# Opening stage of a two-block transformer kernel: modulation as columns on transposed tiles, unit weights by piece, masks by ScalarE and VectorE

## What is computed

```python
# block 1
mod = silu(c) @ w_mod + b_mod                     # 6 rows of 1024: sh1, sc1, gt1, sh2, sc2, gt2
h = layer_norm(x) * (1.0 + sc1) + sh1
proj = h @ w_in                                    # xbc, dt, q, k, v, f, z and two gates
xbc = silu(causal_depthwise_conv(xbc, conv_w, conv_b))
# block 2, used much later, depends on positions only
mod_2 = silu(c_2) @ w_ada + b_ada                  # 6 rows more
bias = bias_table[t5_bucket(pos_k - pos_q)]        # 32 buckets, 24 heads, 256 x 256 each
```

## Time and profile before

| | |
|---|---|
| median of 3 runs | 2214.21 us |
| the profiled execution's own time | 2215.75 us |
| its span, first to last instruction | 2213.9 us |
| mean granted TensorE clock | 0.873 |
| TensorE matmul busy | 1644.6 us (74%) |
| VectorE, ScalarE, GpSimd busy | 440.2, 287.3, 104.3 us |
| DMA | 670.55 MB, mean 303 GB/s |

### The profile page before, as it was taken

The page is one execution under the profiler, slowest core; times in us unless marked ns, Lnnn a source line. Parts: engine busy times, 40 slices in busy tenths (PEclk is TensorE's granted clock), DMA queues, the critical chain, the costliest instruction groups (busy, mean ns, idle before and its releaser), DMA issues.

```text
span 2213.9 us, 19952 instructions
## 1 busy us (share of the span) xinstructions
PE 1644.6 (74%) x8097; PEld 860.0 (39%) x8097; DVE 440.2 (20%) x890; ACT 287.3 (13%) x602; POOL 104.3 (5%) x99
## 2 busy tenths in 40 slices
PE   6899999979998699999998744655464544554444
PEld 2575654444443477687754411311121111211111
DVE  6430542342222322121325300000000000000001
ACT  6211222020000222121223100000000000000000
POOL 7000000000000100111111000000000000000000
PEclk9999999979999799999999777877778766877777
DMA  8899444729998342443452479999999999999995
GB/s 276 293 340 341 178 157 142 295 90 429 426 429 316 128 152 78 166 138 133 137 169 105 200 335 428 428 427 429 427 429 427 428 427 428 427 429 427 428 427 247
DMA packets 116171, 670.55 MB, mean 303 GB/s; under 512 B 8643, under 2 KB 11400, under 8 KB 85360
## 3 DMA queue, kind: packets, MB, share of 16 engines
q1 hardware_dynamic: 111568, 657.50, 73.3%
q0 software_dynamic: 3744, 11.11, 1.7%
q10 hardware_dynamic: 768, 0.64, 0.1%
HBM read 661.88 MB, written 7.34 MB: 302 GB/s over the span
## 4 chain that ended last, share of the span: by engine, by line
PE 61%; DMA 31%; DVE 3%; ACT 2%; issue 2%; SPq 1%; POOL 0%; DVEq 0%; ACTq 0%; POOLq 0%
PE psum L914 13%; PE psum L904 12%; DMA ring<-in_w_up 10%; DMA ring<-in_w_down 10%; PE psum L1403 10%; DMA ring<-in_w_gate 9%; PE psum L1217 5%; PE psum L1247 3%; PE psum L872 2%; PE psum L1187 2%; PE psum L1257 1%; PE psum L1143 1%; SPq L643 1%; PE psum L1340 1%; PE psum L1277 1%
## 5 line engine op out<-in xcount | busy, mean ns | idle before, releaser
L1403 PE MATMUL psum<-work,prob 128*32 128x512 f32 x1024 | 286.5, 724 | 159.0 <-DMA ring<-in_w_up 83.9
L1403 PE MATMUL psum<-ring,prob 128*32 128x512 f32 x1024 | 286.5, 724 | 151.1 <-DMA work<-in_w_up 86.2
L914 PE MATMUL psum<-ring,hT 128*128 128x512 f32 x672 | 303.8, 597 | 4.7 <-ACT hT L177 2.9
L904 PE MATMUL psum<-hT,ring 128*128 128x256 f32 x1152 | 277.2, 385 | 1.6 <-DVE hT L177 1.6
L904 PEld LDWEIGHTS psum<-hT,ring 128*128 128x128 f32 x1152 | 213.7, 193 | 36.3 <-issue 10.6
L1403 PE MATMUL psum<-work,hT 128*32 128x512 f32 x512 | 138.4, 703 | 88.8 <-DMA ring<-in_w_down 88.8
L1403 PE MATMUL psum<-ring,hT 128*32 128x512 f32 x512 | 138.4, 703 | 55.6 <-DMA work<-in_w_down 54.0
L914 PEld LDWEIGHTS psum<-ring,hT 128*128 128x128 f32 x672 | 123.9, 191 | 135.7 <-issue 129.1
L1403 PEld LDWEIGHTS psum<-work,prob 128*32 128x32 f32 x1024 | 70.7, 131 | 261.7 <-issue 261.7
L1403 PEld LDWEIGHTS psum<-ring,prob 128*32 128x32 f32 x1024 | 70.6, 131 | 253.1 <-issue 253.1
L177 ACT ACTIVATE work<-psum 128x512 f32<-128x512 f32 (+2 forms) x99 | 56.0, 566 | 608.3 <-PE psum L1389 236.5
(11 more groups left out here) (322 smaller groups left out, 1581.1 us busy)
## 6 DMA issues: line engine op xcount, KB each, us to landing
ring<-in_w_gate SPq DMA_DIRECT2D x40, 2048.0 KB, 19.2
work<-in_w_up SPq DMA_DIRECT2D x40, 2048.0 KB, 20.4
work<-in_w_gate SPq DMA_DIRECT2D x40, 2048.0 KB, 20.4
ring<-in_w_up SPq DMA_DIRECT2D x40, 2048.0 KB, 20.7
ring<-in_w_down SPq DMA_DIRECT2D x40, 2048.0 KB, 19.8
work<-in_w_down SPq DMA_DIRECT2D x40, 2048.0 KB, 20.0
ring<-in_w_in SPq DMA_DIRECT2D x72, 1024.0 KB, 7.4
ring<-in_w_mod SPq DMA_DIRECT2D x24, 1024.0 KB, 8.9
```

The costliest lines, as they stand in the source:

```text
L904: mm = pe.matmul(o[:, wide(j * S, S)], w[:, ch], actT[:, c, :], start=(c == 0), stop=(c == KC - 1))
L914: mm = pe.matmul(o, actT[:, c, wide(t * P, P)], w, start=(c == 0), stop=(c == KC - 1))
L1403: mm = pe.matmul(o[wide(i * CAP2, CAP2), :], lhs(chunks_per * piece + c, i), R.slot(l + i, (chunks_per, width))[:, c, wide(b * BANK, BANK) ...
```

## The change

* **Modulation as columns.** The spread of units 0 and 1 (four jobs) goes. TensorE instead turns `mod_rows` into columns: 16 matmuls of 64x2 into one bank (job `cols`), from which VectorE makes `mod_cols` (two operations of 128x8). Tokens are only centred and scaled (`centred`, one pass of 128x1024 per tile, without modulation), transposed early, and copied to `hT` by ScalarE. Once the columns are there, the eight channel rows of `hT` (128x256 each) are multiplied and shifted in place, four by VectorE (`hT_low`) and four by ScalarE (`hT_high`).
* **Units by piece.** The four loads of every unit are now two weight rows by 1024 columns each, in place of four rows by 512. TensorE waits for one load at a time, and each piece frees its own slot (`unit_used`, `read`).
* **Positions first.** SyncE issues the positions, then x, before all else; the token positions of the quarters are cut out by VectorE, not loaded. The clearing of `cond` moves to GpSimd.
* **Masks by ScalarE and VectorE.** GpSimd's subtraction goes. ScalarE computes the absolute distance in one activation per query, with the query's position as a bias column (four activations of 128x256 in place of one of 128x1024). The 16 steps are written out; 7 mask buffers (`mask_of`) and 4 staging buffers of two steps each (`BIAS_STAGES`). VectorE copies three halves of every four out of PSUM and ScalarE one. A store covers two steps: four DMAs of 192 KB.
* **Order.** Units 0 and 1, transposes and bias steps are interleaved on TensorE; steps 10 to 15 come after the first xbc chunk and its unit. The loads start before the first store, and stores stand between loads.

The diff, cut to its core:

```diff
+        def read(n):
+            reader = loads[n][2]
+            return reader if isinstance(reader, tuple) else done(reader)
...
         def load_unit(u):
-            for n in range(2):
-                load_chunk(f"unit{u}_{n}", (w_mod, w_ada)[u // 6], wide(u % 6 * D + n * BANK, BANK), job(f"unit{u}"))
+            src = (w_mod, w_ada)[u // 6].rearrange("(p c) n -> p c n", c=KC)[:, :, wide(u % 6 * D, D)]
+            at = len(unit_loads) * 3
+            unit_loads[u] = [load(src[:, wide(2 * i, 2), :], (2, D), job(f"unit{u}") if i == 3 else (unit_used, at + i + 1)) for i in range(4)]
...
+        mask_of = [0, 1, 2, 3, 4, 5, 6, 0, 1, 2, 3, 0, 1, 2, 3, 0]
...
+        def stage_free(eng, s):
+            g = s // 2
+            if s % 2 == 0 and g >= BIAS_STAGES:
+                eng.wait_ge(bias_stored[g % BIAS_STAGES], g // BIAS_STAGES * BIAS_STORES)
...
+            fetch_run(8, 10)
+            store_bias(0)
+            fetch_run(10, 11)
+            store_bias(1)
+            fetch_run(11, 12)
+            store_bias(2)
+            fetch_run(12, 14)
+            store_bias(3)
+            fetch_run(14, 16)
+            store_bias(4)
+            for g in range(5, BIAS_GROUPS):
+                fetch_run(2 * g + 6, 2 * g + 8)
+                store_bias(g)
+            fetch_run(2 * BIAS_GROUPS + 6, moe_load0)
...
-                weights = [dict(pieces(f"unit{u}_{n}")) for n in range(2)]
-                for c in range(KC // 2):
+                for i, load_n in enumerate(unit_loads[u]):
+                    pe.wait_ge(*arrived(load_n))
+                    weights = slot(load_n, (2, D))
                     for n in range(2):
                         for half in range(2):
-                            mm = pe.matmul(o[wide(64 * n + 32 * half, 32), :], cond[:, u // 6, half * (KC // 2) + c, 31 - u:63 - u], weights[n][half * (KC // 2) + c],
-                                           start=(c == 0), stop=(c == KC // 2 - 1))
+                            mm = pe.matmul(o[wide(64 * n + 32 * half, 32), :], cond[:, u // 6, 2 * i + half, 31 - u:63 - u], weights[:, half, wide(n * BANK, BANK)],
+                                           start=(i == 0), stop=(i == 3))
+                            if n == half == 1 and i < 3:
+                                mm.then_inc(unit_used, 1)
...
             pe.wait_ge(signal("table_in"), 64)
-            bias_round(0)
-            with pe.Fori(1, BIAS_ROUNDS) as it:
-                bias_round(it)
-            next_job[0] += BIAS_ROUNDS * BANKS
-            in_one(modulation(0))
-            in_one(modulation(1))
+            bias(0, 1)
             pe.wait_ge(signal("const_in"), 16)
+            transpose_tokens("hT", h, "h_ready", (0,))
+            unit = modulation(0)
+            one_piece(unit)
+            one_piece(unit)
+            bias(2)
+            one_piece(unit)
+            transpose_tokens("hT", h, "h_ready", (1,))
+            one_piece(unit)
+            bias(3)
+            unit = modulation(1)
+            for s in (4, 5, 6):
+                one_piece(unit)
+                bias(s)
+            one_piece(unit)
+            bias(7)
+            pe.wait_ge(*emptied(job("unit1")))
+            o = begin(job("cols"))
+            for c in range(KC):
+                for n in range(2):
+                    mm = pe.matmul(o[wide(64 * n, 64), wide(2 * c, 2)], mod_rows[wide(64 * n, 64), c::KC], select[wide(64 * n, 64), wide(16 * n, 2)], start=True, stop=True)
+            end(mm)
+            bias(8)
...
-            spread(0, 1)
+            bias(9)
+            pe.wait_ge(signal("hT_low"), KC // 2)
+            pe.wait_ge(signal("hT_high"), KC // 2)
+            channel_major("xbc", 1, hT, IN_UNITS["xbc"])
+            bias(10, 11, 12, 13, 14, 15)
+            channel_major("xbc", 4, hT, IN_UNITS["xbc"], 1)
...
+            def distances(*steps):
+                for s in steps:
+                    if mask_free(s):
+                        act.wait_ge(*mask_free(s))
+                    for q in range(BIAS_QUERIES):
+                        ins = a.activation(one_hot[mask_of[s]][:, q, :], pos_all, ACT.Abs, bias=pos_quarter[:, s * BIAS_QUERIES + q:s * BIAS_QUERIES + q + 1])
+                    ins.then_inc(signal("distance_ready"), 1)
...
+            distances(8)
+            act.wait_ge(*emptied(job("cols")))
+            for c in range(KC // 2, KC):
+                step(a.activation, hT[:, c, :], hT[:, c, :], ACT.Identity, bias=mod_cols[:, 0, c:c + 1], scale=mod_cols[:, 1, c:c + 1], signals=(signal("hT_high"), c - KC // 2 + 1))
+            distances(9)
...
                 take(job("xbc", j), u_pad[:, 2 * j:2 * j + 2, 3:3 + S], src=lambda o: o.rearrange("p (c t) -> p c t", c=2))
+                if j == 1:
+                    distances(14)
+                    bias_out(11)
+                    distances(15)
+                    bias_out(13, 15)
...
+            in_bucket(8)
+            bias_out(6)
+            add_row(1)
+            bias_out(7)
+            k = job("cols")
+            dve.wait_ge(*done(k))
...
+                if ct == 3:
+                    bias_out(10)
+                    in_bucket(14)
+                    bias_out(11)
+                    in_bucket(15)
+                    bias_out(12, 13, 14, 15)
```

More of the change, by code:

```diff
@@ L317, in plan_spread, with plan_chunks @@
                 jobs(f"mod{u}", 2)
-        def plan_chunks(name, w, col0, n, units=()):
-            for i in range(n):
+        def plan_chunks(name, w, col0, n, units=(), first=0):
+            for i in range(first, n):
                 jobs(f"{name}_{i}", 2)
@@ L623, in first_free @@
                         last = [next(n for n in range(end - 1, -1, -1) if n % SLOTS == one) for one in (2 * s, 2 * s + 1)]
-                        free.append([done(loads[n][2]) for n in last])
+                        free.append([read(n) for n in last])
                 return free
@@ new lines, in bias_out, with take_hT @@
+            def bias_out(*steps):
+                for s in steps:
+                    stage_free(act, s - 1)
+                    k = job(f"bias{s}", 0)
+                    act.wait_ge(*done(k))
+                    a.activation(staged_half(s, 0), bank(k), ACT.Copy).then_inc(emptied(k)[0], 1)
+            def take_hT(t):
+                for half in range(2):
+                    take(job("hT", 2 * t + half), hT[:, 4 * half:4 * half + 4, wide(t * P, P)], src=lambda o: o.rearrange("p (c t) -> p c t", c=4))
@@ L1506, in _ @@
-            act.wait_ge(signal("const_in"), 16)
-            logs_and_exps()
-            for t in range(TT):
-                rstd_of(t, t)
-            for n in range(2):
-                take(job("mod0", n), mod[:, 0, wide(n * BANK, BANK)])
-            for n in range(2):
-                take(job("mod1", n), mod[:, 1, wide(n * BANK, BANK)], ACT.Identity, bias=1.0)
+            logs_and_exps()
+            rstd_of(0, 0)
+            distances(2)
+            rstd_of(1, 1)
+            distances(3)
@@ new lines, in in_bucket, with bias_out @@
+            def in_bucket(*steps):
+                for s in steps:
+                    dve.wait_ge(signal("distance_ready"), s + 1)
+                    step(v.tensor_scalar, one_hot[mask_of[s]], one_hot[mask_of[s]], bucket_range[:, 1:2], None, ALU.is_le, signals=(signal("one_hot_ready"), s + 1))
+            def bias_out(*steps):
+                for s in steps:
+                    stage_free(dve, s)
+                    for j in range(s % 2, 2):
+                        take(job(f"bias{s}", j), v.tensor_copy, staged_half(s, j), bank(job(f"bias{s}", j)))
@@ L1791, in _ @@
-            for t in range(TT):
-                norm_stats(t, t)
+            centred(0)
+            in_bucket(2)
+            bias_out(0)
+            centred(1)
+            in_bucket(3)
+            bias_out(1)
             step(v.memset, u_pad[:, :, 0:3], 0.0, signals=(signal("pad_ready"), 1))
```

214 lines of the change are left out of this document (107 added, 107 removed).

## The result

The changed kernel takes 2195.8 us (median of four runs, 2195.4 to 2196.7); the kernel before took 2214.4 in runs beside it. The ratio is 0.9914, with a 95% interval of 0.9902 to 0.9926: 18.6 us less, forecast 18.2. The profiled execution took 2195.37, with a span of 2193.6 (before 2215.75 and 2213.9). The total came out almost to the microsecond, but two of its parts did not, as the experiments show.

A forecast was written before the change was run, and what follows sets the result against it. TensorE was taken to bound the opening, transfers the stage from 1226 us. xbc 1 starting at 76.8 instead of 94.97 saves 18.2, all arriving: 2197.6 us profiled, 2196 against the median; range 2190 to 2205.

The forecast's parts named there:

- Step 1: Kernel start: x issued at about 1.3 us, landing at about 7.0; TensorE starts at 9.6, before at 11.96.
- Step 2: TensorE up to the columns: bias 0 to 7, transposes and both units take 25.1 us without waiting, ending at 34.7.
- Step 3: Columns, `mod_cols`, affine, distance 9, mask, bias 9: xbc 0 starts at 46 us, not 74.7, after a nearly 4 us TensorE hole.
- Step 4: First xbc chunk: 16.7 us, not 14.01, with the clock lowered by the hole; ends at 62.7, unit 2 at 66.3.
- Step 5: Bias 10 to 15 after xbc 0 and unit 2: 10.4 us without TensorE waiting; xbc 1 starts at 76.8.
- Step 6: Transfers up to xbc 3's last load: landed at 101 us, wanted at 113, slack 12, so covered.
- Step 7: Removed work such as the spread (3.7 us) adds no gain of its own; units by piece in later stages gain 0.
- The better case: Rival: columns at 1.9 us and xbc 0 at full clock give 1.6 + 2.7 more; gain 22.5, 2192 us; chance 0.15.
- VectorE as the bound: Rival: masks in the opening stay at 1.75 us for a reason other than GpSimd; gain 10, 2204 us; chance 0.12.
- The low clock throughout: Rival: TensorE stays at 1.2 GHz through the opening, losing 28 us; 10 slower, 2224 us; chance 0.05.
- The transfers: Rival: up to xbc 3 the queue moves only 293 GB/s, 17 of the 18 us are gone; 2213 us; chance 0.05.
- doesn't do what it says: Rival: at the start, first weights or x still wait for slow positions, all moves by 5 us; gain 13; no separate chance.

The follow-up runs named there:

- best_x_first: Changed kernel with distance 9 and mask ahead of the columns' wait, GpSimd's small DMAs after x, first mask before statistics, x issued before positions: 2193.0 us.
- gpsimd_busy: Changed kernel with GpSimd also doing 14 subtractions of 128x1024 on memory nobody uses then: 2204.9 us, ratio 0.9953.
- before_spacer: Kernel before the change plus one unused tensor of 64 bytes per partition where the change puts `mod_cols`: 2211.1 us, ratio 0.9983.
- weights_after_x: Changed kernel, but SyncE issues the first eight weight loads only when x has landed: 2194.2 us, ratio 0.9908.
- mask9_early: Changed kernel with distance 9, its mask and ScalarE's copy of bias 7 ahead of the wait for the columns: 2191.4 us, ratio 0.9895.

## Why the prediction was right, step by step

*Step 1, start: too early by 3.1.* x landed at 10.0 and not at 7.0, TensorE started at 12.70 and not at 9.6. The 5.0 that I took from the earlier trace rows was the time of a transfer issued at 6.69, when the consts and positions had landed, and the 7.0 left only 0.7 for its neighbours; 2.0 of the lateness came from the positions' broadcast (`best_x_first`), 0.4 from GpSimd's DMAs, none from the weights, and the rest isn't accounted for.

*Step 2, TensorE to the columns: 26.9 for 25.1.* TensorE was the bound, as forecast, and never waited over 0.2 us. The first two steps took 5.44, at half pace at first, where the sum has 5.2. Each of the six others cost 1.91 where I took 1.73, and a piece 1.00 for 0.9: I had priced them from steps that follow their like (1.75 here too, in the x24 row), while in this order the kind of product changes every time, which adds 0.1 to 0.2 at each change. VectorE's slack was real (16.70 busy of 22 us from 10 to 32), and `gpsimd_busy` shows that it hung on GpSimd's silence.

*Step 3, columns to xbc 0: 11.1 for 11.3, from errors that cancel.* Columns 2.04 (taken 3.5, bound 1.9), `mod_cols` 0.4 (0.8), affine 2.5 (2.5), distance 9 1.60 (1.7), mask 0.77 (0.85). Bias 9 took 3.57 for 1.8.

*Step 4, xbc 0: 13.8 for 16.7.* The mechanism was right, the place wrong. The hole lowered the clock, but the low stretch came on bias 9, which I had priced at full speed, and was over when xbc 0 began. I had charged the whole of it to the first long group behind the hole, as the earlier trace rows shows it, although there was a short one in between. Nor was the hole as long, as step 4 has it: in the kernel before TensorE had three, of 3.59, 1.55 and 1.61, with 3.1 of transposes between them, and the clock read 0.50 from 71 to 80. Here it was one of 3.49, and it cost 1.8 for 2.7. Net it was 1.1 us cheaper than forecast.

*Step 5, bias 10 to 15: 10.5 for 10.4.* No waits. *Step 6, transfers:* no wait for the ring in chunks 1 to 3. *Step 7:* right for the units behind xbc's chunks. The forecast had the transfer-bound stage from 1226 us on; it starts at 1275.51 before the change, which changes nothing in the sum.

*The sum.* The terms together miss by 1.8 at xbc 1 (78.6 for 76.8; gain 16.4 for 18.2). That all of it arrives was nearly right: 16.05 at 1259 us (15.2 to 16.1 over the three executions with the old opening). The last 4.2 come from the place of `work`, which the forecast doesn't contain. So the total is right by luck, because a size 2 too large in the opening met a gain of 4 that wasn't looked for; by its own mechanism the change is worth 14 to 16 us and would have come out at 2198 to 2200.

*The rivals.* The better case got its columns (2.04) and its clock in xbc 0, but not its start. VectorE as the bound happens as soon as its condition is made (`gpsimd_busy`, 2204.9 for 2204 forecast; the nearness is in part luck, since the forecast priced the masks alone). The low clock throughout did not happen: behind the first bias steps TensorE ran at full pace up to the hole. The transfers had 383 GB/s there, near the 388 of the earlier trace rows and far from the slice's mean of 293 that this rival needed. The rival "doesn't do what it says" has a grain of truth: x did lose 2.0 us to the positions, as a transfer beside it.

## What to carry to other kernels

Price a step in the company in which it will run: the same product costs 1.75 among its like and 1.91 between others, and a transfer of 1 MB 5.0 us when issued at 6.69 with little beside it, 8.8 behind a broadcast at the program's start. Where the last step before the heavy work waits in line behind something late (distance 9 behind the affine), its path counts twice, once as time and once as clock, so it is moved first.

And look at where buffers lie before crediting an edit. A new 64-byte tensor moved everything declared behind it, and in a stage of 938 us that the transfers bound this gave 4.2 us, over a quarter of what the edit itself gave. Such a share is told apart by an unused spacer in the old kernel, which is a one-line run.

## What the runs showed of the hardware

- *Place in memory.* 428 and 430 GB/s, 938.4 and 934.1 us, for a shift of 64 bytes a partition of what is declared behind it.
- *GpSimd and VectorE.* A mask of 128x1024 takes 0.75 alone and up to 2.74 beside GpSimd's subtractions, copies from PSUM 0.70 in both cases; four operations of 32x64 took 1.8 in all beside GpSimd's DMA issues and 1.0 without.
- *Start-up.* x (1 MB) landed after 8.8 us behind a broadcast of 128 KB, after 6.4 ahead of it; the weights behind it made no difference, 16 small DMAs of GpSimd 0.4.
- *Clock.* After a hole of 3.5 us TensorE took 3.57 for a step of 1.75, and ran at 1.00 from 50.7 us on. Without the hole the same step took 1.75. At the start the first two bias steps took 5.4 to 6.5 while the granted clock read 1.00. The second `dtf` group and the chunk behind it took 15.8, 17.5 or 19.1 us together, and nothing between, in kernels that are the same there; `before_spacer` has 19.1 where the kernel before has 17.5. The granted clock goes with it: 1.00 in `weights_after_x` (15.8), down to 0.66 in the changed kernel (17.5; 135 to 140 us), 0.50 in `mask9_early` (19.1; 131 to 134). What decides between the three wasn't settled, and a gain of the opening can grow or shrink by 1.7 there.
